# A hybrid attention decoder layer: the attention-times-values product in plain fp32 on paired column halves, two gate weight buffers, and the first norm's root moved behind the projections

## What is computed

```python
h = rms_norm(x, attn_norm)
(mq, mk, mv, nsq, kc, vc, ksl, vsl, kwn, vwn, ngate, mgate) = split(h @ w_in)
y_a = moba_attention(q_a, k_a, v_a)            # 8 heads of 64, blocks of 256
y_b = nsa_attention(q_b, compressed, selected, window)   # 8 heads, 2 key/value groups
x = x + (sigmoid(gA) * (y_a @ W_A) + sigmoid(gB) * (y_b @ W_B)) @ W_o
x = x + gelu(conv_a) * conv_b @ W_down          # causal conv of rms_norm(x) @ W_up
x = x + sigmoid(x @ W_pg) * (p @ W_pp)
```

## Time and profile before

| what | value |
|---|---|
| median of 3 runs | 921.58 us (920.68 to 921.92) |
| profiled execution, its own time | 921.52 us |
| its span, first to last instruction | 919.7 us |
| busy: PE / DVE / ACT / POOL | 884.6 / 423.9 / 411.8 / 437.0 us |
| mean granted TensorE clock | 0.996 |

### The profile page before, as it was taken

How to read it: one execution, slowest core, us unless ns; L and a number is a source line. 1 busy time by engine, 2 the same in 40 slices (tenths; PEclk the granted TensorE clock), 3 DMA queues, 4 the chain that set the end, 5 groups by cost and what they waited for, 6 DMA issues and landing times.

```text
span 919.7 us, 13404 instructions
## 1 busy us (share of the span) xinstructions
PE 884.6 (96%) x4601; PEld 764.8 (83%) x4601; DVE 423.9 (46%) x961; ACT 411.8 (45%) x893; POOL 437.0 (48%) x557
## 2 busy tenths in 40 slices
PE   7999899999899799999999999999999999999998
PEld 7899699999798687877788888888888888888886
DVE  4545665767755654545413644444444440021124
ACT  5224555665646454634333544444444442231321
POOL 4740644664634342656462464444444445444450
PEclk9999999999999999999999999999999999999999
DMA  5845423333121223456532453333333333322213
GB/s 175 198 116 149 104 62 101 93 75 87 47 58 47 58 71 113 138 192 207 180 120 80 157 153 92 103 91 92 92 99 97 97 98 108 99 94 91 92 58 137
DMA packets 101366, 99.33 MB, mean 108 GB/s; under 512 B 15956, under 2 KB 76084, under 8 KB 101300
## 3 DMA queue, kind: packets, MB, share of 16 engines
q1 hardware_dynamic: 101247, 98.48, 36.5%
q10 hardware_dynamic: 53, 0.01, 0.0%
HBM read 87.58 MB, written 10.88 MB: 107 GB/s over the span
## 4 chain that ended last, share of the span: by engine, by line
PE 85%; DVE 5%; ACT 4%; issue 3%; POOL 2%; DMA 1%; SPq 0%; ACTq 0%; DVEq 0%; POOLq 0%
PE banks L1516 25%; PE banks L1517 25%; PE banks L1518 25%; PE banks L1667 2%; PE banks L1647 1%; PE banks L1646 1%; PE banks L1576 1%; PE banks L1604 1%; ACT split_arena L1013 1%; DMA plain_arena<-gates 1%; DMA plain_arena<-in_conv_w_dram 1%; ACT split_arena L889 1%; PE banks L1701 1%; DVE plain_arena L1301 1%; DVE split_arena L1200 1%
## 5 line engine op out<-in xcount | busy, mean ns | idle before, releaser
L1516 PE MATMUL banks<-split_arena 128*128 128x512 f32 (+4 forms) x1228 | 463.1, 377 | 12.8 <-DVE split_arena L1200 6.2
L1518 PE MATMUL banks<-split_arena 128*128 128x512 f32 (+4 forms) x1228 | 453.4, 369 | 0.0
L1517 PE MATMUL banks<-split_arena 128*128 128x512 f32 (+4 forms) x1228 | 453.3, 369 | 0.0
L699 POOL TENSOR_TENSOR split_arena<-plain_arena,split_arena 128x512 fp32r<-128x512 f32 x184 | 241.1, 1322 | 254.8 <-ACT split_arena L941 235.2
L1516 PEld LDWEIGHTS banks<-split_arena 128*128 128x128 f32 x1228 | 231.1, 188 | 50.9 <-DVE split_arena L1200 7.2
L1518 PEld LDWEIGHTS banks<-split_arena 128*128 128x128 f32 x1228 | 230.7, 188 | 35.4
L1517 PEld LDWEIGHTS banks<-split_arena 128*128 128x128 f32 x1228 | 231.3, 188 | 31.9
L941 ACT ACTIVATE split_arena<-plain_arena 128x512 fp32r<-128x512 f32 x184 | 113.0, 627 | 193.2 <-PE banks L1518 179.1
L1474 DVE SCALAR_TENSOR_TENSOR plain_arena<-banks,plain_arena 128x511 f32<-128x511 f32 x44 | 32.7, 743 | 133.2 <-ACT plain_arena L1053 133.2
L900 ACT ACTIVATE plain_arena<-plain_arena 128x128 f32<-128x128 f32 (+1 forms) x96 | 54.0, 562 | 52.7 <-DVE plain_arena L1301 52.4
L714 POOL TENSOR_SCALAR plain_arena<-plain_arena 128x128 f32<-128x128 f32 (+1 forms) x64 | 41.0, 641 | 74.4 <-DVE plain_arena L1318 74.4
(11 more groups left out here) (170 smaller groups left out, 821.7 us busy)
## 6 DMA issues: line engine op xcount, KB each, us to landing
plain_arena<-in_w_up_dram SPq DMA_DIRECT2D x88, 256.0 KB, 3.1
plain_arena<-in_w_down_dram SPq DMA_DIRECT2D x44, 256.0 KB, 2.6
plain_arena<-in_w_in_dram SPq DMA_DIRECT2D x18, 512.0 KB, 4.3
plain_arena<-in_w_in_dram SPq DMA_DIRECT2D x32, 192.0 KB, 4.2
plain_arena<-in_x_dram SPq DMA_DIRECT2D x8, 512.0 KB, 5.4
gates<-plain_arena SPq DMA_DIRECT2D x16, 256.0 KB, 2.0
plain_arena<-skew SPq DMA_DIRECT2D x16, 256.0 KB, 3.9
plain_arena<-gates SPq DMA_DIRECT2D x16, 256.0 KB, 4.2
```

Of the source, the lines that this page charges most:

```text
L699: pool.tensor_tensor(W2l[:, c % RING, :], raw2[:, c % RING, :], W2h[:, c % RING, :].bitcast(F32), ALU.subtract).then_inc(w2_lo, 1)
L1516: nc.tensor.matmul(o, ah, bh, start=first, stop=False)
L1517: nc.tensor.matmul(o, ah, bl, start=False, stop=False)
L1518: return nc.tensor.matmul(o, al, bh, start=False, stop=last)
```

## The change

**Steps.** Within a pair the order is now branch, then head, then query tile. A step is `due` when it is the last of the second head (or the compressed step), so `values` runs 12 times for two heads at once and four times for the compressed keys.

**Values.** `PT` (four unit slots), `V` (a slot for each of pairs 0 to 3, reused later) and `VC` are plain fp32. `pt_low`, `v_high`, `v_low` and the low part of the compressed values are gone; ACT copies the turned probabilities once (`take_probs`), POOL copies V once (`take_values`). For each key tile j two plain products are issued, one with output in partitions 0 to 63 for the first head, one in 64 to 127 for the second, with 64 weight columns each.

**Gates.** `Gh` and `Gl` have two buffers; high and low parts are made one gate earlier, those of gate 3 at step 1, raw weights are loaded one gate earlier. DVE takes the gate out of bank 7, multiplied with the row of roots (`gate_scale`), ACT does the tanh in place, and PE waits for `gate_scaled`.

**Start.** SP loads x tiles 0 and 1, then the weights of unit 0, then x tiles 2 and 3; the seven constant loads move to ACT's queue, in front of its own. Unscaled x is turned in two halves of 256 tokens, tile by tile as it lands; the second half is turned in the middle of `project_first`, before its kt 6. The root is taken later, off the turned x: `take_proj` and the copies of unit 0 multiply by it (`scale=rstd`), and PE spreads it to a row with four plain products (`spread_rstd`), copied out by ACT. The load of projection unit 1 moves ahead of that of the compression weights.

```diff
-        for e in range(2):
-            for br in (["own"] if n < 4 else ["slc", "win"]):
+        for br in (["own"] if n < 4 else ["slc", "win"]):
+            for e in range(2):
...
+        Gh = [r3(14336, KT, P), r3(7296, KT, P, AR)]
+        Gl = [r3(15360, KT, P), r3(8320, KT, P, AR)]
+        PT = AF[:, 0:8192].rearrange("p (u j q) -> p u j q", u=4, j=NT)
+        V = AF[:, 8192:10240].rearrange("p (s t c) -> p s t c", s=4, t=NT)
...
-            def v_low(w):
+            def take_values(w):
                 n = w - 1
+                pool.wait_ge(qkv_done, 4 * w + 4)
+                if n >= 4:
+                    pool.wait_ge(pv_done, (n - 4) // 2 + 1)
+                pool.tensor_copy(V[:, vslot(n)], qkv[:, :, 256:384]).then_inc(v_done, 1)
...
                 for j, end in gate_end.items():
-                    if t == end + 1 and j + 1 < NGATE:
-                        split_gate(j + 1)
+                    if t == end + 1 and j + 2 < NGATE:
+                        split_gate(j + 2)
+                if t == 1:
+                    split_gate(3)
...
-            def pt_high(t):
+            def take_probs(t):
                 s = STEPS[t]
+                u, i = s["u"], s["i"]
                 act.wait_ge(turned, t + 1)
+                if u >= 4:
+                    act.wait_ge(pv_done, values_of[u - 4])
...
             def take_gate(j):
+                act.wait_ge(gate_scaled, j + 1)
+                nc.scalar.activation(gstage, gstage, ACT.Tanh, scale=0.5).then_inc(gate_tanh, 1)
...
+            def gate_scale(j):
+                dve.wait_ge(gate_filled, j + 1)
                 if j > 0:
+                    dve.wait_ge(g_out, 16 * j)
+                nc.vector.tensor_tensor(gstage, PS[:, 7, :], rstd_row, ALU.mult).then_inc(gate_scaled, 1)
+            square_x(1)
+            dve.wait_ge(cst_done, 1)
+            h_low(0)
+            square_x(3)
+            h_low(1)
+            gate_high(0)
+            gate_low(0)
             dve.wait_ge(x_sq, NT)
+            rsqrt(rstd, ssx, 1.0 / D, 4)
...
-                    for j in (reversed(range(NT)) if closing else range(NT)):
-                        q = slice(P * j, S)
-                        ins = three(PS[:, 6, q], Vh[:, vs, j, c0:c0 + P], Vl[:, vs, j, c0:c0 + P], PTh[:, u % 2, j, q], PTl[:, u % 2, j, q],
-                                    opening and j == 0, closing and j == 0)
+                    for j in range(NT):
+                        for h in range(2):
+                            c0 = DH * (h if n < 4 else s["br"] == "win")
+                            ins = nc.tensor.matmul(PS[DH * h:DH * (h + 1), 6, P * j:S], V[:, vslot(n), j, c0:c0 + DH], PT[:, (u - 1 + h) % 4, j, P * j:S],
+                                                   start=opening and j == 0, stop=closing and j == NT - 1)
...
-            warm(20)
+            warm(12)
             turn_consts()
-            warm(16)
-            for kt in range(KT):
-                turn_input(kt)
+            turn_input(0)
+            turn_input(1)
+            warm(8)
             project_first()
             gate(0)
+            spread_rstd()
```

More of the change, by code:

```diff
@@ L78, in layer @@
     NSTEP = [last_t[n] - first_t[n] + 1 for n in range(NPAIR)]
-    unit_last_t = {s["u"]: t for t, s in enumerate(STEPS) if s["last"]}
+    values_count = list(itertools.accumulate(s["due"] for s in STEPS))
+    values_of = {s["u"]: values_count[t] + (not s["due"]) for t, s in enumerate(STEPS)}
     def ucols(w):
@@ L470, in _ @@
         def _(sp):
-            for tt in range(NT):
-                sp.dma_start(xnat[:, tt, :], x_d[tt]).then_inc(x_in[tt], 16)
+            wk = A["w_in"].rearrange("l (k p) n -> p (l k) n", p=P)
+            for half in range(2):
+                for tt in range(2 * half, 2 * half + 2):
+                    sp.dma_start(xnat[:, tt, :], x_d[tt]).then_inc(x_in[tt], 16)
+                if half == 0:
+                    for part in range(2):
+                        ks = slice(4 * part, 4 * part + 4)
+                        sp.dma_start(raw[:, ks, 0:256], wk[:, ks, C_KC:C_KC + 256]).then_inc(raw0_in[part], 16)
+                        sp.dma_start(raw[:, ks, 256:280], wk[:, ks, C_NG:C_NG + 24]).then_inc(raw0_in[part], 16)
             def load_unit(w, kts):
@@ L1202, in _ @@
-            dve.wait_ge(x_in[2], 16)
-            nc.vector.tensor_tensor_reduce(out=R[:, 8192 + 2 * D:8192 + 3 * D], in0=xnat[:, 2, :], in1=xnat[:, 2, :], scale=1.0, scalar=0.0,
-                                           op0=ALU.mult, op1=ALU.add, accum_out=ssx[:, 2:3]).then_inc(x_sq, 1)
-            dve.wait_ge(x_sq, NT)
-            rsqrt(st[:, 80:84], ssx, 1.0 / D, 4)
-            for half in range(2):
-                for tt in range(NT):
-                    part = xnat[:, tt, half * 512:(half + 1) * 512]
-                    nc.vector.tensor_scalar(part, part, st[:, 80 + tt:81 + tt], None, ALU.mult).then_inc(h_nat, 1)
@@ new lines, in square_x, with h_low @@
+            def square_x(tt):
+                dve.wait_ge(x_in[tt], 16)
+                nc.vector.tensor_tensor_reduce(out=square_out[:, tt, :], in0=xnat[:, tt, :], in1=xnat[:, tt, :], scale=1.0, scalar=0.0,
+                                               op0=ALU.mult, op1=ALU.add, accum_out=ssx[:, tt:tt + 1]).then_inc(x_sq, 1)
+            def h_low(half):
+                for kt in range(KT):
+                    q = slice(256 * half, 256 * half + 256)
+                    dve.wait_ge(hT_hi, KT * half + kt // 2 * 2 + 2)
+                    nc.vector.scalar_tensor_tensor(out=hTl[:, kt, q], in0=turned_part(half, kt), scalar=cst[:, kt:kt + 1],
+                                                   in1=hTh[:, kt, q].bitcast(F32), op0=ALU.mult, op1=ALU.subtract).then_inc(hT_lo, 1)
@@ L1700, in warm @@
                 for _ in range(count):
[L1701 removed]
+                    nc.tensor.matmul(PS[:, 1, 0:P], ones, ones, start=True, stop=True)
             def project_first():
@@ L1747, in _ @@
                     turn_probs(t - LAG)
-                if t >= VLAG and STEPS[t - VLAG]["last"]:
+                if t >= VLAG and STEPS[t - VLAG]["due"]:
                     values(t - VLAG)
```

324 lines of the change are left out of this document (149 added, 175 removed).

## The result

The changed kernel takes **923.8 us** (median of 18 runs, 922.0 to 926.2) against 920.9 us for the kernel before (18 runs, 919.2 to 922.7): a ratio of **1.0029, 95% interval 1.0020 to 1.0038**. It is slower by 0.3%, a little more than the 0.2% that can be told from no change. The forecast was 901.8 us, and faster. The profiled execution took 923.4 us with a span of 921.5 us, so the two traces, 919.7 against 921.5 us, differ by 1.7 us as a pair.

The account below looks back on a forecast made before the run. PE, busy 884.6 of 919.7 us, plus some stalls was taken to bound the kernel. 921.5 - 16.3 - 1.5 - 6.2 + 1.0 - 0.7 + 4.0 = 901.8 us; own range 894 to 909, eight in ten 892 to 928.

Parts of the forecast that it names:

- Values, -16.3: Values calls: plain products paired on array halves cost PE 33.3 us in place of 49.6, a gain of 16.3 us.
- The lower bound: Values call: 2.13 us if both array halves work at the same time, against 4.27; 2.45 with slots, entry and exit.
- drain at a change of tiling mode: Values calls: if each mode change drained TensorE for 178 ns, 24 entries and exits would cost 4.3 us, not 2.2.
- Gate waits, -6.2: Gates: with a second buffer, all 6.2 us of PE's waits for the low part of gate weights go.
- zero, and up to the 0.7 us of the multiplication a gate if it were not: Gates: cost of the multiplication's wait in DVE's queue for the previous gate's spill DMA, taken as zero.
- Start, -0.7: Start: earlier first projection but hardly earlier vector transposes, 0.7 us gained, between +1 and -4.
- which I also put at 24 to 25: Start: time in us of DVE's low part of the second half, after which gate 0's high part is made.
- From 400 us on, 0: Stretch from 400 us to the end: left alone by the change, same length to 1 us.
- What comes back, +4.0: Chains ending in normalised tiles: less PE work hides them, so a quarter of the gain returns, 4.0 us, ends 0 and 12.
- PE runs into the chains: Rival for the steps: halves overlap, but step chain and roots bind; 12 us come back, 909.8 us; chance 0.13.
- One head after the other: Rival for values calls: halves do not overlap, a call takes 4.72 us, kernel taken as 928 us; chance 0.21.
- two signs named for a wrong forecast: Values call longer than 3 us, or PE's idle time in the steps not falling below 18 us.

Follow-up runs that it names:

- e3: Changed kernel with the two loops of a values call exchanged, all of one head's products before the other's: 941.5 us, ratio 1.0222 to the kernel before.
- e7: Changed kernel with one gate buffer again, gate parts and raw weights made when they were before: 930.2 us, ratio 1.0087 to the kernel before.
- e6: Changed kernel with its whole start undone and no DVE multiplication of the gates; values and two gate buffers kept: 918.9 us, ratio 0.9967.
- e10: Kernel of e9 with the gate's multiplication put ahead of the bias in DVE's queue: 911.6 us, ratio 0.9891 to the kernel before.
- e8: Changed kernel with DVE making gate 0's weight parts before the low part of the second half of h: 917.6 us, ratio 0.9959.
- e5: Changed kernel with the plain arena cut to 14272 columns, making the operand distance 0 modulo 128 bytes: 919.0 us, ratio 0.9973.
- e1: Changed kernel with 8 more columns in the plain arena (14288): 920.3 us, ratio 0.9990 to the kernel before.
- e4: Changed kernel with 8 and 11 unused plain products before the first and third vector transposes: 921.5 us, ratio 1.0002 to the kernel before.
- e11: Kernel of e9 with plain products of no use put where PE stalls: 910.5 us, ratio 0.9882 to the kernel before.
- e9: Changed kernel with 14272 columns in the plain arena and gate 0's weights first on DVE: 912.7 us, ratio 0.9906 to the kernel before.

## Why the prediction was wrong

Against the profiled executions the forecast missed by 21.6 us. By its own terms:

- **Values, -16.3.** Right, at 15.4. The call was 2.30 us from first product to the next kind; with entry and exit it costs 2.50, where 2.45 was counted. The lower bound was the right one to take, for the reason given (e3). The Trainium skill's drain at a change of tiling mode ("TensorEngine Tiling (Array Packing)", "Key Properties"), counted there as 4.3 us for 24 changes, would have its trace in the entries, 0.17 us longer than those of a split product, 1.9 us for eleven; the traces don't tell whether it is a drain, and 0.08 us of it is there before a compressed product on the full array as well.
- **Gate waits, -6.2.** The waits for the weights went (e7 brings them back), but only half of the 6.2 us was gained. Behind them stood a second condition of the same gates, that bank 7 is empty, which the forecast put at "zero, and up to the 0.7 us of the multiplication a gate if it were not". After the change PE waits 3.1 us for it, on the multiplication, and without the multiplication 4.8 us, on the tanh (e6). The multiplication stands behind the bias, which in a compressed step is three operations, one after the other; ahead of the bias it is not waited for (e10).
- **Start, -0.7: it was +5.6.** The step that failed is "which I also put at 24 to 25". The low part of the second half ended at 26.3. I had said that POOL's table hangs on it, gave +1 as the end of the range, and did not follow the other engines: POOL's copies, 1.7 us later, then lay against DVE's subtractions, one of which took 5.2 us, and the low clock came on top. e8 gained it all back by the order of two calls.
- **From 400 us on, 0: it was +3.5**, with another 1.7 ahead of it (e5). "The change does not touch these, apart from names" was false: it moved operands into another arena. The diff showed that; what an address may cost no row showed.
- **What comes back, +4.0.** The idle time of PE was to fall from 20.3 to 17.6 and stayed at 19.6, so this was short by 2.0, the bank 7 waits among it. The waits that grew are not the ones named: normalised tiles stood at 5.7 us instead of 8 to 10, and the growth is in L789, L841 and L1220.
- **The clock, no term.** Low clock between first score and the second root grew by 13.7 us; PE was at work in 12.9 us of it, which makes 6.0 us of time, an estimate by the 0.47. It is the largest part of what failed in the steps. With 1.00 and 0.99 in the earlier trace rows I read the clock as given. The stalls are not more than before: of over 1 us there are 6 between 86 and 405 us, where there were 8. Why one of 1.4 us now brings the lower level (347.8) and those of 1.4 us before the change did not stays open.

Steps and middle were to shrink by 19.0 us and shrank by 7.3. Of the 11.7 missing, 6.0 are the clock, 2.0 idle time, 1.7 the layout, 0.9 the values; 1.1 stay open. Adding start (6.3) and late stretch (3.5) gives 21.5. None of the rivals held. "PE runs into the chains" would have left 25.6 us of idle time. "One head after the other", at 928, is nearest in the number, and the range up to 928 holds the result only because it was stretched for that rival; with a call of 2.30 us this is luck. Of the two signs named for a wrong forecast one came (idle time not below 18 us); the sound call length shows that the main mechanism held.

For the start it is shown that the low clock hangs on the stall in front: each of the five traces with PE's wait of 2.9 us at 40 to 44 us has 6.8 us of it at 41 to 43 (after, e1, e3, e5, e7), and none of the others has any there (filled in e4, gone in e8). For the steps it is less certain. Filling (e11) or removing (e10) a stall took the stretch behind it away (in e11 two others came, behind waits of 2.2 and 2.0 us), but in e4 one went and two grew with their stalls unchanged. How long a stall must be is not shown; at 109 us e9 has 1.4 and 0.7 us of idle time, and no low clock follows in its trace.

## What to carry to other kernels

When a change takes work from the engine that is always busy, price the stalls twice: once as idle time and once for the clock that may fall behind them. When a wait is taken away, look for the next condition of the same instruction, which the list of waits doesn't show. For each instruction added to a queue ask what stands before it there, not only what it waits for. And treat a move of operands as a change with a cost until the distance between products of the trace says otherwise.

## What the hardware showed unexpectedly

- The distance between a product's two operands in memory matters. For 512 columns of fp32r the products are 227 ns apart when its remainder by 128 bytes is 0 (and in the kernel before), 226 to 232 when it is 64 and 233 to 234 when it is 32 (products with an operand in `late_arena`). Four layouts are all that shows it.
- One DVE subtraction with two operands in SBUF took 5.21 us in place of 0.56, beside some nine instructions of POOL.
- Plain fp32 products on separate column halves overlap fully: starts 7 ns apart, and pairs of 384 columns follow one another after 322 ns, as single ones do in e3. A values call starts 0.17 us later behind a transpose than a split product does.
